# Recurrence of a two-block model: the inverse multiplied from the right, and exclusive sums over time as a second product on TensorE

## What is computed

```python
def wkv_scan(r, decay, k, v, a_vec, b_vec, s0, reverse):
    def step(s, inp):
        r_t, w_t, k_t, v_t, a_t, b_t = inp
        sa = jnp.einsum('bhvk,bhk->bhv', s, a_t)
        s = s * w_t[:, :, None, :] + sa[..., None] * b_t[:, :, None, :] + v_t[..., None] * k_t[:, :, None, :]
        return s, jnp.einsum('bhvk,bhk->bhv', s, r_t)
```

## Time and profile before

| | |
|---|---|
| median of 3 runs | 2923.95 us (2920.44 to 2925.3) |
| span of the profiled execution, first to last instruction | 2917.6 us |
| median of the runs above that span | 6.35 us |
| PE, VectorE, ScalarE, GpSimd busy | 91%, 47%, 34%, 6% |
| mean granted TensorE clock | 0.964 |
| DMA moved, mean | 717 MB, 246 GB/s |

### The profile page before, as it was taken

One profiled execution on the slowest core, in us unless ns is written; L12 is line 12 of the kernel. 1 busy time (PEld: TensorE's weight loads), 2 busy tenths in 40 slices (PEclk: granted clock), 3 DMA queues, 4 the chain that ended last, 5 costly groups with the idle time before them and its releaser, 6 DMA issues.

```text
span 2917.6 us, 56415 instructions
## 1 busy us (share of the span) xinstructions
PE 2663.8 (91%) x24182; PEld 1779.7 (61%) x24182; DVE 1366.9 (47%) x1878; ACT 983.7 (34%) x1705; POOL 189.3 (6%) x195
## 2 busy tenths in 40 slices
PE   8999999999999999999999998899999989766666
PEld 6877877878878878875433333344778865332222
DVE  5776566877866567643100001423777773000001
ACT  4435655444446555531200100202555542000000
POOL 0102000000002000000000000002333310000000
PEclk9999999999999999999999999999999999987787
DMA  8764335776763347642899999822100017999997
GB/s 304 274 258 161 127 131 210 302 267 244 297 236 135 125 166 286 229 176 107 346 421 421 421 421 421 328 81 101 42 11 17 11 47 282 421 421 421 421 419 323
DMA packets 103997, 716.99 MB, mean 246 GB/s; under 512 B 11949, under 2 KB 14381, under 8 KB 19801
## 3 DMA queue, kind: packets, MB, share of 16 engines
q1 hardware_dynamic: 93016, 663.75, 57.8%
q10 hardware_dynamic: 10752, 49.81, 4.5%
HBM read 711.65 MB, written 1.86 MB: 245 GB/s over the span
## 4 chain that ended last, share of the span: by engine, by line
PE 61%; DMA 20%; DVE 10%; ACT 6%; issue 2%; SPq 0%; ACTq 0%; DVEq 0%
DMA weight_ring<-in_stream 20%; PE banks L2130 9%; PE banks L667 7%; PE banks L669 6%; PE banks L668 6%; PE banks L1960 3%; PE banks L2495 3%; PE banks L1103 3%; PE banks L1105 2%; PE banks L1104 2%; PE banks L2539 2%; ACT front L1371 2%; PE banks L1263 1%; PE banks L2935 1%; PE banks L2021 1%
## 5 line engine op out<-in xcount | busy, mean ns | idle before, releaser
L2130 PE MATMUL banks<-weight_ring,scratch 128*32 128x256 f32 (+1 forms) x4256 | 560.3, 507 | 148.6 <-DMA weight_ring<-in_stream 147.0
L2130 PEld LDWEIGHTS banks<-weight_ring,scratch 128*32 128x32 f32 (+1 forms) x4256 | 183.1, 129 | 505.9 <-DMA weight_ring<-in_stream 258.7
L664 DVE TENSOR_TENSOR split_high<-weight_ring,split_high 128x1024 fp32r<-128x1024 f32 x198 | 242.5, 1238 | 124.0 <-ACT split_high L659 121.8
L659 ACT CAST split_high<-weight_ring 128x1024 fp32r<-128x1024 f32 x198 | 206.8, 1052 | 272.8 <-PE banks L669 199.3
L2281 DVE TENSOR_TENSOR scratch<-scratch,banks 128x512 f32<-128x512 f32 (+1 forms) x32 | 17.8, 555 | 561.5 <-PE banks L2130 561.5
L1463 DVE TENSOR_TENSOR split_high<-weight_ring,split_high 128x1024 fp32r<-128x1024 f32 x128 | 160.2, 1262 | 160.9 <-ACT split_high L1356 160.8
L667 PE MATMUL banks<-split_high,features_low 128*128 128x512 f32 x480 | 189.9, 396 | 0.2 <-DVE resid L700 0.2
L669 PE MATMUL banks<-split_high,features_high 128*128 128x512 f32 x480 | 187.1, 390 | 0.0
L668 PE MATMUL banks<-split_high,features_high 128*128 128x512 f32 x480 | 186.8, 389 | 0.0
L1356 ACT CAST split_high<-weight_ring 128x1024 fp32r<-128x1024 f32 x128 | 133.0, 1049 | 150.1 <-PE banks L1105 144.2
L2190 ACT ACTIVATE scratch<-banks 128x512 f32<-128x512 f32 (+1 forms) x32 | 15.7, 491 | 477.7 <-PE banks L2130 477.7
(11 more groups left out here) (448 smaller groups left out, 4870.2 us busy)
## 6 DMA issues: line engine op xcount, KB each, us to landing
weight_ring<-in_stream SPq DMA_DIRECT2D x628, 1024.0 KB, 9.8
scratch<-in_kept ACTq DMA_DIRECT2D x24, 1024.0 KB, 7.6
scratch<-in_pair_rows ACTq DMA_DIRECT2D x8, 448.0 KB, 3.7
scratch<-in_kept ACTq DMA_DIRECT2D x6, 512.0 KB, 5.5
scratch<-in_lora ACTq DMA_DIRECT2D x2, 1536.0 KB, 9.3
front<-in_gain_rows ACTq DMA_DIRECT2D x5, 512.0 KB, 3.7
bias<-bias_rows SPq DMA_DIRECT2D x1, 2304.0 KB
scratch<-in_routing ACTq DMA_DIRECT2D x1, 1040.5 KB, 4.9
```

The source lines that it names most:

```text
L659: act.copy(split[i % 4][0], source(i)).then_inc(*self.rounded.up())
L664: dve.tensor_tensor(lo, source(i), hi.bitcast(F32), ALU.subtract).then_inc(*self.rest.up())
L2130: last = pe.matmul(self.psum[q * M:(q + 1) * M, (GATE, UP, DOWN)[part], 0:W], left, w[j][:, q * W:(q + 1) * W], start=(k == 0), stop=(k == ...
```

## The change

The equations are rearranged. Before, X was multiplied by (`AW`) the `a` rows and by the product of the key scores with the values (`lak_values`, copied to `W`), and the two results (`GW`) then met `Bt`, `Lr` and the values in `mt`, `kv`, `ht` and `y_inside`. After, X multiplies from the other side: `qr` computes X with `Bt` and with the b part of the query scores (`QR`); `mth` multiplies that by `At` and so gives the chunk matrix and the query correction in one product; `kl` multiplies it by the key scores `Lak`, and VectorE adds the result to the keys `Kt` and to the key part of the query scores `Lr` (`add_keys_inside`). `kv` and `y_inside` then need the values only once.

The scores are grouped anew: `scores_a` is AT against both BT and KT (products of 128 columns), `scores_b` is BT against AT and the queries and KT against the queries. The part that begins X now comes from `scores_a`, and `Lab` from `scores_b`. The exclusive sums come from a second product with a strict mask, written to bank 2, while the inclusive ones go to bank 0; `exclude` is gone. The `y_state` products of a unit all move to the next step. The order of the calls in all engines' loops changes. The core of the diff, with functions that are only removed and semaphore names left out:

```diff
             def sums(u):
                 d = u % 2
                 pe.wait_ge(w_tanh.sem, u + 1)
-                if u >= 2:
-                    pe.wait_ge(lakv_saved.sem, u - 1)
-                pe.matmul(self.psum[:, F[2], :], incl_sum[d], th_w, start=True, stop=True).then_inc(*sums_incl.up())
+                pe.matmul(self.psum[:, F[0], :], incl_sum[d], th_w, start=True, stop=True).then_inc(*sums_incl.up())
                 pe.wait_ge(a_added.sem, u + 1)
                 for t in range(4):
                     last = pe.matmul(self.psum[:, F[1], 2 * t:2 * t + 2], th_w[:, cols(t)], self.halves, start=True, stop=True)
                 last.then_inc(*sums_all.up())
+                if u >= 3:
+                    pe.wait_ge(k_added.sem, u - 2)
+                elif u == 1:
+                    pe.wait_ge(pex_ready.sem, 1)
+                pe.matmul(self.psum[:, F[2], :], excl_sum[d], th_w, start=True, stop=True).then_inc(*sums_excl.up())
...
+            def turn_queries(u):
+                pe.wait_ge(rt_ready.sem, u + 1)
+                if u < units - 1:
+                    pe.wait_ge(pex_ready.sem, u + 2)
+                else:
+                    pe.wait_ge(k_added.sem, u - 1)
                 for t in range(2):
                     last = pe.transpose(self.psum[:, F[2], cols(t)], rt[:, cols(t)], ident[:, :])
...
+            def scores_a(u):
+                pe.wait_ge(k_saved.sem, u + 1)
                 for t in range(4):
                     for h, c in quads:
+                        at_ = slice(t * P + c * HD, t * P + c * HD + HD)
+                        out = self.psum[half(c), F[h ^ c], :].rearrange("p (n x) -> p n x", n=2)[:, :, t * HD:(t + 1) * HD]
+                        last = pe.matmul(out, AT[half(h), at_], BKT[half(h), :, at_], start=True, stop=True)
+                last.then_inc(*scored_a.up())
+
+            def scores_b(u):
+                d = u % 2
+                pe.wait_ge(lak_masked.sem, u + 1)
...
             def z(u, n):
                 d = u % 2
                 if n == 1:
-                    pe.wait_ge(x_begun.sem, u + 1)
+                    pe.wait_ge(lab_saved.sem, u + 1)
...
+            def qr(u):
+                d, n = u % 2, u % 3
                 pe.wait_ge(x_placed.sem, 5 * u + 5)
-                pe.wait_ge(lakv_saved.sem, u + 1)
+                pe.wait_ge(lr_masked.sem, u + 1)
                 if u:
                     pe.wait_ge(state_ready.sem, 7 * u)
...
+            def kl(u):
+                pe.wait_ge(qr_saved.sem, u + 1)
+                if u:
+                    pe.wait_ge(y_saved.sem, u)
+                bank = F[2] if u < units - 1 else F[0]
...
+                        last = pe.matmul(out, Lak[u % 2][half(c), g, t, :], qr_of(c, g, t), start=True, stop=True)
+                last.then_inc(*kl_ready.up())
...
             for s in range(2, units + 4):
...
+                if b is not None:
+                    qr(b)
                 if l is not None:
                     z(l, 1)
                 if e is not None:
-                    y_state(e, 6)
-                if b is not None:
-                    gw(b)
-                if l is not None:
-                    dx(l, 1)
-                    lak_values(l)
-                    z(l, 2)
-                if b is not None:
-                    mt(b)
-                if e is not None:
-                    y_state(e, 7)
-                if l is not None:
-                    dx(l, 2)
+                    for n in range(4, 8):
+                        y_state(e, n)
                 if g is not None:
                     logits(g)
                 if s == units + 2:
                     output_gates()
+                if l is not None:
+                    dx(l, 1)
                 if b is not None:
-                    kv(b)
-                    ht(b, 0)
+                    mth(b)
+                if l is not None:
+                    z(l, 2)
+                if b is not None:
+                    kl(b)
+                if l is not None:
+                    dx(l, 2)
+                if g is not None:
+                    sums(g)
                 if l is not None:
                     z(l, 3)
                 if b is not None:
-                    ht(b, 1)
-                if g is not None:
-                    sums(g)
+                    kv(b)
                 if l is not None:
                     dx(l, 3)
                 if b is not None:
                     step(b, 1)
-                    y_inside(b)
+                if f is not None:
+                    turn_queries(f)
+                    turn(f, 0)
                 if l is not None:
                     z(l, 4)
                 if b is not None:
                     step(b, 2)
                 if f is not None:
-                    turn(f, 0)
                     turn(f, 1)
+                    turn(f, 2)
                 if l is not None:
                     dx(l, 4)
                 if b is not None:
                     step(b, 3)
                 if f is not None:
-                    turn(f, 2)
+                    scores_a(f)
...
+                    y_inside(b)
...
                 if f is not None:
-                    scores_kr(f)
+                    scores_b(f)
                 if b is not None:
                     step(b, 6)
```

VectorE. `begin_x` waits for `scored_a` in place of `lab_saved`, and `mask_lr` for `lab_saved`:

```diff
+            def add_keys_inside(u):
+                n, d = u % 3, u % 2
+                bank = F[2] if u < units - 1 else F[0]
+                dve.wait_ge(kl_ready.sem, u + 1)
+                dve.tensor_tensor(Kt[n][:, 0:256], self.psum[:, bank, 0:256], Kt[n][:, 0:256], ALU.add)
+                dve.tensor_tensor(Kt[n][:, 256:512], self.psum[:, Y, 256:512], Kt[n][:, 256:512], ALU.add)
+                inside = Lr[d][:, :, 0:2, :]
+                dve.wait_ge(lr_masked.sem, u + 1)
+                dve.tensor_tensor(inside, self.psum[:, bank, 256:512].rearrange("p (g t c) -> p g t c", g=2, t=2), inside, ALU.add)\
+                    .then_inc(*k_added.up())
...
             for s in range(units + 4):
...
                 if l is not None:
-                    masks(l)
+                    mask_lr(l)
+                if e is not None:
+                    save_y(e)
                 if l is not None:
                     place(l, 1)
                     turn_x(l, 2)
-                if e is not None:
-                    save_y(e)
-                if l is not None:
-                    place(l, 2)
-                    turn_x(l, 3)
                 if g is not None:
                     add_offsets(g)
...
                     save_mt(b)
                     save_ht(b)
+                if l is not None:
+                    place(l, 2)
+                    turn_x(l, 3)
+                if b is not None:
+                    add_keys_inside(b)
...
                     place(l, 3)
                     turn_x(l, 4)
                 if g is not None:
-                    exclude(g)
+                    directions(g)
+                if f is not None:
+                    sum_bonus(f)
                 if l is not None:
                     place(l, 4)
                     turn_x(l, 5)
+                if g is not None:
+                    decay_r(g)
                 if f is not None:
                     begin_x(f)
+                    mask_lak(f)
                 if l is not None:
                     place(l, 5)
```

ScalarE. In its loop the copy of `Lab` for unit l is now the first thing in a step, ahead of `save_z(l, 1)`; the three copies of `QR` are of 384 columns where those of `GW` were of 512:

```diff
                     save_z(l, 3)
+                if g is not None:
+                    decays(g)
                 if b is not None:
                     state(b, 0)
                 if g is not None:
-                    decays(g)
+                    chunk_decays(g)
                     if g % 2 == 0 and 2 <= g < units - 2:
                         load_rows(g // 2 + 1)
+                if g is not None:
+                    exclusive_decay(g)
                 if b is not None:
                     state(b, 1)
+                if f is not None:
+                    save_r(f)
+                    if f < units - 1:
+                        act.wait_ge(sums_excl.sem, f + 2)
+                    copy(AT, self.psum[:, F[0], :], turned_a, f + 1, a_saved)
                 if l is not None:
                     save_z(l, 4)
```

More of the change, by code:

```diff
@@ new lines, in scores_b @@
+            def scores_b(u):
+                d = u % 2
+                pe.wait_ge(lak_masked.sem, u + 1)
+                for t in range(4):
+                    for h, c in quads:
+                        at_ = slice(t * P + c * HD, t * P + c * HD + HD)
+                        out = self.psum[half(c), F[h ^ c], t * HD:(t + 1) * HD]
+                        if t < 2:
+                            pe.matmul(pair(out, out.offset + 384), BT[half(h), at_], ART[d][half(h), :, at_], start=True, stop=True)
+                        else:
+                            pe.matmul(out, BT[half(h), at_], AT[half(h), at_], start=True, stop=True)
+                for t in range(2):
+                    for h, c in quads:
```

(23 more changed lines are left out.)

229 lines of the change are left out of this document (93 added, 136 removed).

## The result

The changed kernel takes 2988.3 us (median of 4 runs, 2976.82 to 2994.03), the kernel before on the same chip 2922.3 (2920.44 to 2925.3). The ratio is 1.0224, 95% interval 1.0201 to 1.0248: slower, 10 us above the forecast of 2978 and inside the range of 2935 to 3020. The profiled execution took 2987.64 us, with a span of 2985.8 against 2917.6, thus 68.2 us more.

A forecast was written before the change was run, and what follows sets the result against it. No engine full; a loop handed from engine to engine sets the recurrence's step. Order 33 us plus TensorE's clock 21 us gave 54 on the 2917.6 span, 2971.6; with 6.35 for the median, 2978, range 2935 to 3020.

The forecast's parts named there:

- steps (1) to (16): One recurrence step after the change, walked from `begin_x` to `begin_x`: 24.3 us, 2.5 above 21.75.
- steps (1) to (8): From `begin_x` to the start of `place(1)`: masks, scores, `qr`, `z(1)`, `y_state`s, `logits`, `dx(1)`; 7.73 us.
- (16): End of the step: `place(4)` 0.53, half-size `turn_x(5)` 1.0, `decay_r` 0.33; 1.86 us.
- the edge: From the scores' end to `place(1)`, (3) to (8): 5.2 us, against 2.9 today.
- steps (2) and (6): (2): `scores_b` after its mask, 1.2 us; (6): four `y_state`s standing together ahead of `logits`, 0.93 us.
- Step (12): `add_keys_inside`, 1.1 us; PE's exclusive sum newly waits for it, with `z(3)`, `kv`, `dx(3)`, `step(1)` behind.
- Step (14): `z(3)` until its copy, then ScalarE's `save_z(3)`, `decays`, `state(0)`, `chunk_decays`, `exclusive_decay` in written order: 3.27 us.
- the bound of 62: Clock's upper bound: everything from the exclusive sum to `scores_a` at 1.2 GHz, 4.8 us a step, 13 steps.
- Clock holds: Rival: TensorE keeps full clock, only the order's 33 us are added, 2957 us; chance 0.22.
- The clock is down for the whole second half: Rival: second half of each step at the slow clock, 13 x (2.5 + 4.8) = 95 us, 3019; chance 0.18.
- Faster: Rival: the step's edge costs no more than now and the exponential is hidden, step 20.6 us, 2909; chance 0.14.
- No change: Rival: keys added before PE asks for the bank, step 22.2 us, 6 us at most, 2929; chance 0.06.

The follow-up runs named there:

- run 8: Two kernels: run 7 with four products that nothing reads ahead of `kv`, 2908.42 us, ratio 0.9980; run 2 with `logits` behind `dx(1)`, 2932.75 us, ratio 1.0059.
- run 2: Changed kernel with six products that nothing reads in PE's wait for the keys' sums ahead of the exclusive sum: 2950.6 us, ratio 1.0100.
- run 4: Changed kernel with ScalarE's `decays` moved ahead of `save_z(3)`: 2973.99 us, ratio 1.0180.
- run 10: Changed kernel with three products that nothing reads in another PE wait, ahead of `qr`: 2993.11 us, ratio 1.0270.
- run 5: Changed kernel, exclusive sum behind `dx(3)` and `logits` behind `dx(1)`: 2922.95 us, ratio 1.0010; with the step's second half also reordered on PE and ScalarE: 2914.93, 0.9972.
- run 6: Kernel before with the exclusive sums as a second TensorE product in place of VectorE's subtraction: 2936.9 us, ratio 1.0057.
- run 7: Changed kernel with the exclusive sums by VectorE's subtraction behind `keys`, in place of the product: 2937.38 us, ratio 1.0053.

## Why the prediction was right, point by point

**The account.** In us a step, from pairs of runs: the new order with the subtraction, 21.11 - 21.75 = -0.64 (run 8); the product in that order with the two waits that come with it, of PE for the keys and of `turn_queries` for the exponential, 23.59 - 21.11 = +2.48 (runs 2 and 8, which also differ in where the useless products stand); the clock behind its wait, 26.49 - 23.59 = +2.90 (run 2). Together that is the whole difference, 4.74 over 15 steps, 71 us. Runs 2 and 8 were on chips on which the kernel before differs by 5 us, 0.35 a step, which is how far the first two terms can be trusted.

**The walk, steps (1) to (16).** It gave 24.3 us at full clock; run 2, which has that order and that clock, took 23.59 on average and 23.87 in the step shown. By legs in that step: `begin_x` to `place(1)`, steps (1) to (8), 7.10 against 7.73; to `place(2)`, (9) and (10), 4.28 against 4.04; to `place(4)`, (11) to (15), 10.50 against 10.63; to `begin_x`, (16), 1.99 against 1.86. What the edge was too long by stands in steps (2) and (6). PE shows it in the next step of run 2, which begins at 2211.02:

```profile
2212.37 0.67 PE L2909 MATMUL banks<-scratch 64*64 64x128 f32 x16 [0.19 <-DVE scratch L3133]
...
2213.32 0.30 PE L3013 MATMUL banks<-scratch 64*64 64x64 f32 x4
...
2215.70 0.66 PE L3019 MATMUL banks<-scratch 128*64 128x128 f32 x8
2216.28 1.16 PE L2846 MATMUL banks<-scratch 64*128 64x128 f32 x16
2217.38 0.67 PE L2936 MATMUL banks<-scratch 64*64 64x32 f32 x32
```

`scores_b` takes 0.95 us to the start of `step(6)` and not 1.2; the four `y_state`s take 0.58 to the start of `logits` and not 0.93; `logits` holds PE 1.10 us to the start of `dx(1)`, as walked, though moving it gave only 0.78 (run 8). Step (12), the new wait, was there as named: 1.85 us, ended by `add_keys_inside`. Step (14) fits: `decays` ahead of `save_z(3)` gave its 12 us, with the clock a little higher (run 4). The order thus costs 1.84 us a step and not 2.5; 15 steps of it are 28 us, the forecast had 33.

**The clock** is the term that was mis-sized: "I take a third, 1.6 us, 13 x 1.6 = 21 us". It measured 2.90 a step and 43 us, between that and the bound of 62. The share was the error: in the step shown the leg from `place(2)` to `place(3)` is 7.89 us instead of 5.99 and that to `place(4)` 5.67 instead of 4.51, together 3.06 of the bound's 4.8, thus nearly two thirds. The fall covered the exclusive sum (2.00 us instead of 1.05), `z(3)`, `turn_queries`, `turn(0)`, `z(4)`, `step(2)` and about half of `turn(1)` and `turn(2)` (1.51 to the start of `dx(4)` instead of 1.02); `dx(4)` takes 0.67 as at full clock. The forecast came within 10 us all the same, in part by luck: its order term was 5 us too large and its clock term 22 too small, and the median lies 2.5 us above the profiled span here and not 6.35.

The Trainium skill, "TensorE: Matmul & The Clock Gate", Part 1, that the slow clock is the default and activity releases it, agrees in direction: products without use brought the clock back in runs 2 and 8. That by this rule a wait like (12) would pull the clock down in every step was my inference and is not what the Trainium skill says there; run 10 shows the wait without the fall.

**Where the signs stood.** As forecast: full engines nowhere, no wait ahead of `begin_x`, over 1 us ahead of `place(1)`, the DMA-bound rest unchanged. Ahead of `save_y` I had over 1 us too; it is 0.78, in the changed kernel and in run 2. Ahead of `place(3)` I had about 2.5 us and ahead of `place(4)` about 2: with the clock up they are 2.41 and 1.39 (run 2), with it down 4.32 and 2.73.

**The rivals.** *Clock holds*, 2957: run 2 is that case and took 2950.6. *The clock is down for the whole second half*, 3019: in the step shown the fall ends ahead of `dx(4)`, and its price is 2.90 and not 4.8. *Faster* needs an edge of no more than 4.0 us; run 8 came below the kernel before with the edge about as long as forecast, by shorter legs behind it, and run 5 by `logits` out of the edge and another order of PE and ScalarE behind it. *No change*, the keys added before PE asks, was walked at 22.2; no run is that case, the nearest, without the product, took 21.11 (run 8).

**Open.** Why the clock holds behind the same 1.85 us in some steps of run 10's profiled execution, and why the other four, of which no trace was kept, were 20 us longer.

## What to carry to other kernels

When an instruction moves to an engine that runs in order, ask which wait it brings and what stands behind it there: a product of 0.96 us cost 0.96 us a step where PE did not stand ahead of it (run 6), and 2.48 plus 2.90 of clock where it did. Put a late-fed product behind the work that needs nothing from it, before counting the change as a loss. Where TensorE must stand in a loop anyway, a few products that nothing reads are a cheap test of what the clock costs there; in another wait of the same kernel they changed nothing in four of five executions (run 10).

## What the hardware showed that was not expected

Around a wait of 1.85 us TensorE fell to 1.2 GHz for long enough to cost 2.90 us a step, more than the wait itself; six 128x128 products into unused columns brought 38 us back. In five steps of run 7 `kv` ran at 1.2 GHz behind a wait of 1.25 us, and four such products in that wait raised the clock of the recurrence from 0.85 to 0.98 (run 8).

VectorE's `decay_r`, 128x256 from two tiles in SBUF, takes 0.42 us, but in about every second step of the changed kernel 0.94 to 1.23. In the step shown it starts while a GpSimd product that reads SBUF runs, and ends 0.28 us behind it (2201.50 + 1.23 against 2201.18 + 1.27); in four other steps it ends 0.27 to 0.29 us behind the same product:

```profile
2201.18 1.27 POOL L3513 TENSOR_TENSOR resid<-scratch 128x512 f32<-128x512 f32 x1
```

The Trainium skill, "SBUF — State Buffer", Who interferes with whom, says that a VectorE instruction with two inputs in SBUF contends with a GpSimd instruction that reads SBUF, and that issue order decides who blocks; the rows agree. I had 0.33 us for it in step (16); some 0.65 us in six of the steps was missing there, 0.26 a step. In run 2 it takes 0.54 us in most steps, 0.10 a step more than 0.42, which is why 0.16 of the 2.90 us above is not the clock.
